# Gated attention levels: exponents from 128-row interval sums on TensorE, compact scores, one filler product per unit

## The reference

```python
cum = jnp.cumsum(gc.astype(jnp.float32), axis=1)
inter = jnp.einsum("blhk,bhkv->blhv", qc * jnp.exp(cum), s)
diff = cum[:, :, None] - cum[:, None, :]
decay = jnp.exp(jnp.where(mask[None, :, :, None, None], diff, -jnp.inf))
att = jnp.einsum("bihk,bjhk,bijhk->bhij", qc, kc, decay)
intra = jnp.einsum("bhij,bjhv->bihv", att, vc)
```

## Time and profile before

| what | us |
|---|---|
| median of 3 runs | 3476.84 (3476.39 to 3479.95) |
| profiled execution, its own time | 3473.43 |
| its span | 3471.6 |
| PE, DVE, ACT, POOL busy over the span | 3310.9, 1896.5, 1403.5, 257.4 |
| stage of the 32 levels (from the first fillers at 597.62 to the product with w_out at 735.28) | 137.66 |

### The profile page before, as it was taken

One profiled execution on the slowest core, in us unless ns is written; L12 is line 12 of the kernel. 1 busy time (PEld: TensorE's weight loads), 2 busy tenths in 40 slices (PEclk: granted clock), 3 DMA queues, 4 the chain that ended last, 5 costly groups with the idle time before them and its releaser, 6 DMA issues.

```text
span 3471.6 us, 45331 instructions
## 1 busy us (share of the span) xinstructions
PE 3310.9 (95%) x17843; PEld 2635.8 (76%) x17843; DVE 1896.5 (55%) x2490; ACT 1403.5 (40%) x2239; POOL 257.4 (7%) x265
## 2 busy tenths in 40 slices
PE   6799887899999999999999999999999999999999
PEld 6576655777778878789965559999999655687887
DVE  6777587856534443536565564454545645644433
ACT  4532454444332332324435553343334355533322
POOL 1000033310000000000021000010000300000000
PEclk9999988999999999999999999999999999999999
DMA  6444201014333234323210112342342001123333
GB/s 238 155 152 159 69 22 58 13 61 154 93 118 121 85 98 161 100 87 119 90 43 7 36 40 80 98 162 84 122 148 72 34 7 43 38 90 124 113 91 115
DMA packets 95893, 321.40 MB, mean 93 GB/s; under 512 B 11248, under 2 KB 12672, under 8 KB 95168
## 3 DMA queue, kind: packets, MB, share of 16 engines
q1 hardware_dynamic: 75392, 246.52, 22.3%
q0 software_dynamic: 18752, 67.71, 5.6%
q10 hardware_dynamic: 1536, 4.26, 0.3%
HBM read 295.26 MB, written 23.20 MB: 92 GB/s over the span
## 4 chain that ended last, share of the span: by engine, by line
PE 82%; DVE 11%; ACT 4%; DMA 1%; issue 1%; POOL 0%; DVEq 0%; ACTq 0%; POOLq 0%
PE psum L146 80%; DVE mixer L175 4%; DVE mixer L185 2%; PE psum L149 2%; DVE wlo L175 1%; DVE arena L175 1%; DVE junk L189 1%; DVE mixer L202 1%; ACT whi L163 1%; DVE region L175 0%; DMA mixer<-in_wm 0%; DVE stage L175 0%; ACT mixer L154 0%; ACT arena L154 0%; DMA stage<-in_wi 0%
## 5 line engine op out<-in xcount | busy, mean ns | idle before, releaser
L146 PE MATMUL psum<-region,whi 128*128 128x260 f32 (+2 forms) x7616 | 1833.8, 334 | 6.5 <-DVE region L185 3.2
L146 PEld LDWEIGHTS psum<-region,whi 128*128 128x128 f32 (+1 forms) x7616 | 1278.8, 186 | 173.3 <-DVE region L175 9.6
L146 PE MATMUL psum<-region,wlo 128*128 128x260 f32 (+2 forms) x3808 | 1265.8, 332 | 0.0
L175 DVE TENSOR_TENSOR wlo<-stage,whi 128x1024 fp32r<-128x1024 f32 (+2 forms) x454 | 512.7, 1129 | 639.1 <-ACT whi L163 601.8
L146 PEld LDWEIGHTS psum<-region,wlo 128*128 128x128 f32 (+1 forms) x3808 | 711.2, 187 | 78.5
L163 ACT CAST whi<-stage 128x1024 fp32r<-128x1024 f32 (+2 forms) x454 | 442.2, 974 | 247.3 <-PE psum L146 160.0
L154 ACT ACTIVATE arena<-psum 128x512 f32<-128x512 f32 (+2 forms) x412 | 193.5, 470 | 722.0 <-PE psum L146 717.4
L146 PE MATMUL psum<-arena 128*128 128x512 f32 (+11 forms) x1072 | 382.4, 479 | 0.0
L163 ACT COPY arena<-psum 128x260 f32<-128x260 f32 (+9 forms) x345 | 154.4, 447 | 370.1 <-PE psum L146 353.7
L175 DVE TENSOR_TENSOR arena<-arena 128x512 f32<-128x512 f32 (+8 forms) x341 | 212.2, 622 | 139.9 <-ACT arena L154 129.0
L175 DVE TENSOR_TENSOR arena<-arena,psum 128x512 f32<-128x512 f32 (+1 forms) x220 | 126.2, 574 | 283.7 <-PE psum L146 275.7
(11 more groups left out here) (155 smaller groups left out, 2868.3 us busy)
## 6 DMA issues: line engine op xcount, KB each, us to landing
stage<-in_w SPq DMA_DIRECT2D x144, 512.0 KB, 3.5
stage<-in_wi SPq DMA_DIRECT2D x55, 512.0 KB, 4.4
stage<-in_wo SPq DMA_DIRECT2D x48, 512.0 KB, 3.6
stage<-in_wg SPq DMA_DIRECT2D x44, 512.0 KB, 3.4
stage<-in_wu SPq DMA_DIRECT2D x44, 512.0 KB, 3.4
stage<-in_wm SPq DMA_DIRECT2D x42, 512.0 KB, 3.5
stage<-in_wd SPq DMA_DIRECT2D x32, 512.0 KB, 3.4
arena<-xr_scratch POOLq DMA_DIRECT2D x5, 2080.0 KB, 9.7
```

Source lines behind the costliest of these rows:

```text
L146: return Issued(self, self.e and self.e.matmul(out, w, x, start=start, stop=stop, skip_group_check=True))
L175: return Issued(self, e and e.tensor_tensor(out, a, b, op))
```

## The change

**Exponents.** The differences of `cum` are no longer formed on DVE. A constant 128x128 matrix for each level and direction says which rows lie between a row and its border; TensorE multiplies the gates of a block (128 rows by 128 channels, the weights) by it. `pool_intervals` builds these matrices on POOL at the start of the stage before, and they go through a scratch tensor `IS` to where they are used; the gates `gtk` go through `GS`. The work is cut into 64 units, `PARTS_OF_LEVELS`: 4 groups (q4, f) by 4 parts p (level 64 alone; 32 and 16; 8 and 4; 2 and 1) by 4 blocks jj. `pe_part` computes one filler product and two products (128 moving columns in part 0, 256 in the others) into one bank of (2, 3, 4, 5); `act_part` takes the exponent straight from PSUM (128x256 or 128x512) into `expo`, which is double buffered by part. Two units enter in a round, four before the first.

**Scores.** At each level only the two quarters of 64x64 that matter are computed: 16 products of 64 by 64, 64 columns each. They fill a pair of half-used banks, and that pair is now the only one (`among=(0, 1)`). DVE masks 128x512 (it was 128x1024) into `attc`; ACT copies level 64 only; POOL places `attc` into `att` once for each group of 8 levels (`placed`).

**Order.** The five fillers of a level go; the blocks of outputs start at rounds 19, 23, 27 and 31 (19, 22, 25 and 28 before), with one bank for the transposes; the exponents of q are spread over four rounds. `dve_weights` for `w_out` now waits for the last `placed`.

```diff
-    OUT_AT = {19: 0, 22: 1, 25: 2, 28: 3}
-    Q_AT = {3: 0, 27: 1}
+    OUT_AT = {19: 0, 23: 1, 27: 2, 31: 3}
+    Q_AT = {0: (0, 0), 1: (0, 1), 2: (1, 0), 5: (1, 1)}
...
+    def pool_intervals(e):
+        G, S = sgla.pool, C["m64"]
+        e.wait_ge(*gin2["lvc"])
+        for l, Bs in enumerate((1, 2, 4, 8, 16, 32, 64)):
+            if l == 0:
+                e.tensor_copy(S, C["ident"]).then_inc(*G.up())
+            else:
+                e.tensor_tensor(S, S, C[f"m{Bs // 2}"], ALU.add).then_inc(*G.up())
+            for d, sides in enumerate((("gt", "le"), ("ge", "lt"))):
+                for two, c in enumerate(sides):
+                    a, b = (x.rearrange("p (g two b) -> p two g b", two=2, b=Bs)[:, two] for x in (S, C[c]))
+                    e.tensor_tensor(made[:, d, 6 - l, two * 64:two * 64 + 64].rearrange("p (g b) -> p g b", b=Bs), a, b,
+                                    ALU.mult).then_inc(*G.up())
+        G.mark("intervals")
+        e.wait_ge(*G["intervals"])
+        e.dma_start(IS, made).then_inc(*ist.up("out", by=16))
+        e.tensor_tensor(lvc[:, :, 0:64], lvc[:, :, 0:64], lvc[:, :, 64:128], ALU.add).then_inc(*G.up("compact"))
...
+    def pe_part(e, u):
+        T, A = sgla.pe, sgla.act
+        g, p, jj = PARTS_OF_LEVELS[u]
+        q4, f = divmod(g, 2)
+        b, free = bank.take(("part", u), A, "ex", u, among=(2, 3, 4, 5))
+        for x in free:
+            e.wait_ge(*x)
+        if u % 32 == 0:
+            e.wait_ge(*ivd[q4]["in"])
+            e.wait_ge(*gld[q4]["in"])
+        e.matmul(psum[:, b, 0:128], C["ident"], C["ident"], True, True)
+        for d in range(2):
+            c = sums_of[q4][:, d, max(2 * p - 1, 0):2 * p + 1, :]
+            out = psum[:, b, 0:512 if p else 256].rearrange("p (x d c) -> p x d c", d=2, c=64)[:, :, d, :]
+            ins = e.matmul(out, gq[q4][:, jj, (2 * d + f) * 128:(2 * d + f + 1) * 128], c, True, True)
+        ins.then_inc(*T.up("part", u))
+
+    def act_part(e, u):
+        T, A, D, G = sgla.pe, sgla.act, sgla.dve, sgla.pool
+        g, p, jj = PARTS_OF_LEVELS[u]
+        if jj == 0 and u >= 8:
+            for Bs in {0: (8, 4), 1: (2, 1), 2: (64,), 3: (32, 16)}[p]:
+                n = 8 * ((u - 8) // 16) + [x[1] for x in LEVEL[0:8]].index(Bs)
+                e.wait_ge(*G["qs", n])
+                if Bs > 1:
+                    e.wait_ge(*D["ks", n])
+        e.wait_ge(*T["part", u])
...
-        b, free = bank.take(("yo", j), D, "yo", j, n=2, align=2, among=(4, 5) if j < 4 else (4, 5, 6, 7))
+        b, free = bank.take(("yo", j), D, "yo", j, n=2, align=2, among=(6, 7) if j < 4 else (4, 5, 6, 7))
...
-                b, free = bank.take(("lv", n), A if whole(n) else D, "lv", n, n=2, align=2, among=(0, 1, 2, 3))
+                b, free = bank.take(("lv", n), A if Bs == 64 else D, "lv", n, n=2, align=2, among=(0, 1))
...
                 for jj in range(4):
-                    for hf in range(2):
-                        r_, js = slice(hf * 64, hf * 64 + 64), slice(jj * 128, (jj + 1) * 128)
-                        ins = e.matmul(psum[:, b + hf, js], ks[r_, js], qs[r_, js], True, True)
+                    for kh in range(2):
+                        for hf in range(2):
+                            r_, k0 = slice(hf * 64, hf * 64 + 64), jj * 128 + kh * 64
+                            q0 = jj * 128 + (1 - kh if Bs == 64 else kh) * 64
+                            ins = e.matmul(psum[kh * 64:kh * 64 + 64, b + hf, jj * 64:jj * 64 + 64],
+                                           ks[r_, k0:k0 + 64], qs[r_, q0:q0 + 64], True, True)
...
-        if r == NL + 1:
+        if r == NL + 3:
+            e.wait_ge(*sgla.pool["placed", 3])
             dve_weights(e, W, W.last["wo", 0, 0])
```

More of the change, by code:

```diff
@@ L507, in mixer @@
     K.yd = [K.sig(f"y_in{i}") for i in range(2)]
+    gst, gld, ivd = ([K.sig(f"{n}{i}") for i in range(2)] for n in ("gates_out", "gates_in", "intervals_in"))
+    ist = K.sig("intervals_out")
     def xp(m):
@@ L1436, in sp_ssd @@
         stored_rz(e)
+        for t in range(2, 10):
+            e.wait_ge(*sgla.dve["gtk", t])
+            e.dma_start(GS[:, t - 2, :], gtk[t % 5]).then_inc(*gst[t > 4].up(by=16))
+        for c in gst:
+            c.mark("end")
         e.wait_ge(*sssd.pe["states"])
@@ L1482, in act_states @@
             if k == 0:
+                if i == 0:
+                    e.wait_ge(*gst[1]["end"])
                 if i >= 2:
@@ L1542, in level_in, with compact, att_block @@
         return s, lo, f, Bs, q4, ql, kl
[L1545 to L1550, removed]
+    def compact(n):
+        b = bank.of["lv", n]
+        return psum[:, b:b + 2, 0:256].rearrange("p a (j c) -> p a j c", c=64)
+    def att_block(n, ks, qs):
         f, Bs, q4 = LEVEL[n]
[L1552 to L1558, removed]
+        return att[ks * 64:ks * 64 + 64, f, :, q4 * 4:q4 * 4 + 4, qs * 64:qs * 64 + 64]
@@ new lines, in last_part, with q_planes, k_planes, part_sums @@
+    def last_part(n):
+        return 16 * (n // 8) + 4 * PART_OF[LEVEL[n][1]][0] + 3
+    def q_planes(n, Bs):
+        return expo_of(n)[:, 256:768].rearrange("p (two g b) -> p g two b", two=2, b=Bs)
+    def k_planes(n, Bs):
+        return expo_of(n).rearrange("p (pl n) -> p pl n", n=256)[:, 0:4:3, :].rearrange("p two (g b) -> p g two b", b=Bs)
+    def part_sums(u):
+        p = PARTS_OF_LEVELS[u][1]
+        w = psum[:, bank.of["part", u], :]
+        if p == 0:
+            return w[:, 0:256].rearrange("p (q c) -> p q c", c=64)
+        return w.rearrange("p (l q c) -> p l q c", l=2, c=64)
@@ L1626, in pe_turn @@
         T, A, D = sgla.pe, sgla.act, sgla.dve
-        b, free = bank.take(("turn", j), D, "out", j, among=(6, 7) if j < 4 else (2, 3))
+        b, free = bank.take(("turn", j), D, "out", j, among=(6,) if j < 4 else (2, 3))
         for x in free:
@@ L1708, in act_round @@
         if r in Q_AT:
-            q4 = Q_AT[r]
-            for d in range(2):
-                e.wait_ge(*sssd.pe["end"])
-                e.activation(qc[q4][:, d], cum[:, d * 2:d * 2 + 2, 256 + q4 * 512:768 + q4 * 512], ACT.Exp).then_inc(
-                    *A.up("q", q4, d))
+            q4, d = Q_AT[r]
+            e.wait_ge(*sssd.dve["end"])
+            if q4 and d:
+                for c, last in ((ogd[0], 6), (ogd[1], 7)):
+                    e.wait_ge(*c[last])
+            e.activation(qc[q4][:, d], cum[:, d * 2:d * 2 + 2, 256 + q4 * 512:768 + q4 * 512], ACT.Exp).then_inc(
+                *A.up("q", q4, d))
         for what, j in outputs_at(r):
```

176 lines of the change are left out of this document (99 added, 77 removed).

## The result

Median of four runs 3498.78 us (3492.74 to 3505.85), beside the kernel before 3476.61 (3474.92 to 3479.95): ratio 1.006, interval 1.0042 to 1.0079. The kernel is slower by 22 us, where +8 was forecast; the profiled execution of after took 3494.65, 21.2 more than that of before.

What follows compares the result with a forecast made beforehand. The prediction took DVE to set the pace of the levels, traded for an equal bound on PE. Stage +2.4, clock +2 and intervals +3.5 made +7.9, against the median 3476.84 + 8 = 3485 us; range 3465 to 3504.

Steps and rivals of the forecast that it cites:

- +2.4 and +2 for the stage: Stage of the levels: 140.1 us against 137.7, +2.4; a further +2 from the clock on 122 us of PE work.
- the intervals: POOL's interval matrices in the stage before: 12.4 us of POOL work slowing DVE there, +3.5 us (0 to 8).
- the first rival: Small products at 0.025 us, DVE and POOL not colliding, PE alone counting: groups 23.0, stage 123, kernel near 3466; chance 0.20.
- Bound: Level stage: DVE's pace before; afterwards PE work of 25.3 us for eight levels, 27.3 with waits, against 25.65 before.
- The round: PE's work per level round: level 1.09 us plus two units of 1.12, 3.33 us; 2.67 with part 0 units.
- The collision: DVE's product with k and POOL's with q start together in the level stage; DVE's takes 1.58 us instead of 0.69.
- The chain of 3.65 us: From level to level through DVE's product with k and masked copy: 3.65 us, deciding behind m = 2, 3, 4, 7 of eight.
- The output blocks: Output work at the end of the level stage: `pe_yo`, turns, two waits and DVE's delays, 22.3 us in sum.
- two waits of 2.1: Output blocks 1 and 2: `pe_yo` waits for `dve_out`, with `act_out` behind ACT's two units; 2.1 us each, 4.2 together.
- The clock: Granted clock of the level stage: mean 0.87 before, 0.96 with PE busy nearly throughout; +2 us.
- The tail: End of the level stage, level 31 to the product with w_out: level, copy, POOL's two placing copies, `wlo`; 5.4 us.
- the much slower rival: Quarter-size level products not overlapped, 0.053 or 0.068 us a record, +19 or +35 us: kernel 3504 to 3518; chance 0.16.

Runs made afterwards that it cites:

- e6: Changed kernel with ACT's level 64 copy ahead of the round's first exponent, and its ssd cast and `act_out` at the round's head: 3474.90 us, ratio 0.9992 to before.
- e3: Changed kernel with ACT's cast of the ssd half and `act_out` at the head of its round, ahead of exponents and squares: 3481.70 us, ratio 1.001 to before.
- e2: Changed kernel with ACT's copy of level 64 ahead of the round's first exponent instead of behind it: 3490.39 us, ratio 1.0028 to before.
- e8: Changed kernel with all steps of the output blocks moved behind the last level: 3504.06 us, ratio 1.0078 to before.
- e5: Changed kernel with the edits of e1, e2 and e3 together: 3469.49 us, ratio 0.9978 to before.
- e4: Changed kernel without the 64 filler products at the head of the units: 3489.91 us, ratio 1.0031 to before.
- e7: Changed kernel with the three edits of e5 and without the 64 fillers: 3455.69 us, ratio 0.9943 to before.
- e9: Kernel before, with ACT's copies of large levels and its ssd cast and `act_out` ahead of the round's exponents: 3464.94 us, ratio 0.9965 to before.
- e10: Changed kernel with the two ACT queue moves of e6, without fillers, one pair of banks for levels: 3462.51 us, ratio 0.9956 to before.
- e1: Changed kernel with two pairs of PSUM banks for the levels and two banks instead of four for the units: 3483.62 us, ratio 1.0012 to before.

## Why the prediction was right or wrong

The direction and the range were right, the size was not: +2.4 and +2 for the stage where it was +23.0, +3.5 for the intervals where it was +0.2 to +1.6. That 3498.78 lies in the range, 5 us under its upper end, is luck: the end at 3504 was put there for small products at 0.053 us a record and more, and they take 0.020. Of the first rival (3466) both premises came true, a level under 0.9 us and no collision that costs DVE time; neither it nor the forecast had the waits that decide.

**Bound (right in kind).** From DVE's pace to TensorE's: eight levels without output work take 26.29 us (638.11 less 611.82), forecast 27.3, before 25.65. That the first halves are equal, 61.9 and 62.1, looks like the forecast's trade of equal against equal and is a coincidence of two things that it didn't have, cheap levels and ACT's stops. In e6, where such a stop is 0.8 us at most, eight levels take 23.4 (DVE's products with k start at 608.70 and 632.08) and the first half 57.95, at a clock of 1.00: the first rival's group of 23.0.

**The round (a level mis-sized).** Units were sized right: filler 0.22 and products 0.87, 1.09 in all (forecast 1.12). A level is 0.63 us, not 1.09; 20 ns a record lies even below my lower bound of 25. I had named two halvings of the present level's 0.068, half the moving columns and four quarters of the array instead of two, and took one, 0.034; both give 0.017, near what is measured. Rounds are therefore 3.0 us (654.60 to 657.60), not 3.33.

**The collision (wrong).** I let DVE's product with k take 1.58 beside POOL's, from the earlier trace rows. It stays at 0.69, and POOL pays:

```profile
633.74 0.69 DVE L175 TENSOR_TENSOR mixer<-mixer 128x512 f32<-128x512 f32 x1 [2.30 <-PE psum L146]
```
```profile
633.78 1.78 POOL L175 TENSOR_TENSOR mixer<-mixer 128x512 f32<-128x512 f32 x1 [0.91 <-PE psum L146]
```

DVE starts 0.04 us ahead here. In the earlier trace rows POOL was the first, and where it is first in the changed kernel, DVE is the slow one again:

```profile
678.08 1.41 DVE L175 TENSOR_TENSOR mixer<-mixer 128x512 f32<-128x512 f32 x1
```
```profile
677.66 1.28 POOL L175 TENSOR_TENSOR mixer<-mixer 128x512 f32<-128x512 f32 x1 [8.25 <-PE psum L146]
```

No pair of the stage goes another way: DVE takes 0.69 in each where it starts ahead, and 1.41 and 1.62 in the two where POOL does. How little decides is seen in e3, where POOL starts at 702.40 and takes 1.27, DVE at 702.44 and takes 1.78. I read one row for the size and not for who had begun. The chain of 3.65 us thus never decides.

**The wait I missed on ACT.** Four stops of 2.07 us: level 64's copy stands behind the exponent of the unit that TensorE computes last ahead of the stop (e2). I had priced ACT by its durations (two exponents a round) and did not ask what its queue stands for. With the slower clock behind it this made up for part of the cheap levels: level 17 starts 62.1 us into the stage, where the forecast's terms (8.8, two groups of 27.3, a round of 3.33) give 66.7.

**The output blocks (the step that failed).** The forecast took 22.3 us for them: `pe_yo` at 4.1 each and two waits of 2.1. The two waits came as forecast, 1.98 and 2.19 us. What failed is "DVE's scaling and casts delay some chains, 2". From level 18 to level 26 there are 59.0 us (666.96 to 725.96), where 27.3, two blocks of 4.1 and the two waits, some 40, were forecast. DVE's queue stands for ACT's cast, and with it the masked copy for which TensorE stops, up to 4.8 us at once. e3 takes the cast and `act_out` ahead, and the same eight levels take 41.7 us (669.23 to 710.95), nearly the forecast; the stage is 18.0 shorter, 29.0 in e6 with both moves. e8 shows from the other side that the levels alone go through in 104.6.

**The clock (wrong sign).** I took a rise from 0.87 to 0.96 and got a fall to 0.83. The second half ran at 0.72; TensorE stood still often there, and the work behind most of these stops shows the times of the lower level. From the change to e5 the stage's windows shrink by 33.3 us: idle time from 31.5 to 12.7, busy time from 129.1 to 114.6 for the same products. So somewhat under half of what the stops cost was the slower clock behind them; I had priced waits by their length only. That the stops bring the lower clock, and not it the stops, is shown by the order edits: they touch ACT's queue alone, and the clock of the stage goes from 0.83 to 0.88 in e3. The fillers hold the clock up a little where TensorE stops often (0.83 with them, 0.78 in e4 without) and hardly where it doesn't (0.93 and 0.92 in e5 and e7), and both times the stage is shorter without them.

**The intervals (too dear, by two errors of opposite sign).** POOL takes 0.45 us in the mean for each of the 28 products, 0.5 with the gap to the next, not 0.30, and is at them, the sums and the copy from 409.00 to 430.0:

```profile
409.37 2.07 POOL L175 TENSOR_TENSOR mixer<-hold,mixer 128x64 f32<-128x64 f32 x4
411.52 0.45 POOL L175 TENSOR_TENSOR hold<-hold 128x128 f32<-128x128 f32 x1
```

The path of TensorE lost some 0.3 us for 18.0 of POOL's busy time: the product that stood at 446.44 stands at 447.32, and 0.58 of that it was late at 401 already. Over all traces that stretch takes 45.2 us in both without the intervals, 45.4 to 45.8 in six with them and 46.7 in four. DVE's products of 128x512 between 409 and 430 take 712 ns in the mean, 692 before: the loss of the earlier trace rows does not carry over to these small pieces.

**The tail (right).** Level 31 to w_out (750.15 to 756.10) is 5.95 us, forecast 5.4; before it was 2.69 (from 732.59). The loads were not late, as forecast: the first unit follows the stage before without a stop.

**The rule weighed.** By the rows the small product costs 20 ns. The Trainium skill, "TensorE: Matmul & The Clock Gate", section "Wait — 56ns, not 53.3ns?", has a floor of some 25 ns and one of 62 with decoding by software; the trace is below both, so the much slower rival had no ground in the small products. Its records are of products in four different quarters of the array; whether 20 ns would hold within one quarter, no run here shows.

**Whether the change pays.** Against before it costs 22 us; but so much of this is ACT's order that the fair rival is e9, before with the same two moves. With them the changed levels are slower (e6 131.6, e5 127.3 of the stage) than the old ones (125.7), and the ratios, 0.9992 and 0.9978 against 0.9965, point the same way, though the intervals of the last two overlap (0.9969 to 0.9988, 0.9952 to 0.9977). Only without the fillers are they ahead, 117.9 and 0.9943 in e7; the interval of that ratio ends at 0.9957 and that of e9 begins at 0.9952, so the lead over e9 is likely and small, some 8 us by the stage. e10, which ran beside e9, is ahead by 4.2 us of the stage, and their ratios, 0.9956 and 0.9965, can't be told apart. One rival is untested: e9 keeps its own fillers, five to a level, and what the old levels do with the two moves and without fillers was not run. The first rival's stage of 123 us, TensorE alone, is nearly reached with three edits that the change lacks (127.3). The tail of some 3 us over before was not taken on.

The start of the stage moves between 593.9 and 601.6 us among kernels whose code ahead of it is the same. A part of it is a step: from the product at 446 to the last products ahead of the stage (596.10 before, 593.96 in the changed kernel) it is 149.6 to 150.0 us in seven traces, both kernels with the old levels among them, and 146.5 to 146.7 in the other five, with nothing between. What makes the step is open. Stages are compared by their length for that reason, and since each is of one execution, differences of 3 to 4 us between them (the second pair of banks) are weakly shown. The intervals of the ratios are 6 to 13 us wide, from end to end.

## What to carry to other kernels

When work is taken off the engine that sets the pace, list for each queue what the next instruction waits for, not only how long its instructions last: here an exponent held a copy back until TensorE had done its next unit, 2 us each time, and a cast behind an exponent and four squares held DVE for 15. A copy that frees banks belongs ahead of work that waits for a later event. Price a stop of TensorE at more than its length: in e1, e2, e3, e5 and e6 each microsecond of idle time that went took 0.2 to 0.9 of busy time with it. And try the order edit on the old kernel too before the new layout gets the credit.

## What the runs showed of the hardware

- 32 records of float32 products, 64 rows by 64 weight columns with 64 moving, in four different quarters of the array, follow each other at 20 ns at the full clock (0.63 us), less than a third of the 68 ns for 64 rows by 128 columns with 128 moving. At the lower clock 1.07 us (676.41 to 677.48), 33 ns.
- DVE and POOL on 128x512 elements with both operands in on-chip memory: with DVE 0.04 us ahead DVE takes 0.69, as alone, and POOL 1.78; with POOL 0.42 ahead POOL takes 1.28, as alone (1.28 at 668.13), and DVE 1.41; with POOL 0.04 ahead (e3) 1.27 and 1.78. So the one that starts later pays.
- POOL's product of 128x64 elements takes 0.45 us in the mean of 28, where its sum of 128x128, twice the elements, takes 0.45 to 0.98 and 0.55 in the mean of six. The products read every other group of columns; whether that is the reason was not tried.
- TensorE's clock: behind the stops of 2.07 and 4.79 us at 666.96 and 676.41 a unit's two products took 1.91 us instead of 1.03, and behind that of 1.98 at 687.16 the 24 records of `pe_yo` 7.25 instead of 4.19; behind those of 2.07 at 638.11 and 2.80 at 706.07 a unit's took 1.03 as always. A filler at the head of each unit did not prevent the lower clock. In e8's output blocks TensorE was busy 38.3 of 62.8 us, and the granted clock was 0.50 all the way.
